# A mixture of 32 experts streamed from HBM: the fullest expert in one pass of 128 slots at a fixed place

## The reference

```python
def moe(h, w_router, b_router, w_gate, b_gate, w_up, b_up, w_down, b_down):
    logits = jnp.dot(h, w_router, preferred_element_type=jnp.float32) + b_router
    top_logit, top_idx = lax.top_k(logits, TOP_K)            # TOP_K = 4 of 32 experts
    gates = jax.nn.softmax(top_logit, axis=-1)
    ...
    def expert_block(args):                                  # xb: the tokens of one expert
        xb, e = args
        g = jnp.minimum(xb @ w_gate[e] + b_gate[e], SWIGLU_LIMIT)
        u = jnp.clip(xb @ w_up[e] + b_up[e], -SWIGLU_LIMIT, SWIGLU_LIMIT)
        act = g * jax.nn.sigmoid(SWIGLU_ALPHA * g) * (u + 1)
        return act @ w_down[e] + b_down[e]
    ...                                                      # sum over the 4 choices, times gate
```

## Time and profile before

| what | value |
|---|---|
| median of 3 runs | 1698.13 us (1698.03 to 1700.2) |
| profiled execution, span | 1695.8 us |
| PE busy | 1612.9 us, 95% |
| VectorE (DVE), ScalarE (ACT) busy | 392.1 us, 277.9 us |
| DMA | 524.72 MB, 309 GB/s over the span |
| granted TensorE clock, mean | 0.997 |

### The profile page before, as it was taken

One profiled execution on the slowest core, in us unless ns is written; L12 is line 12 of the kernel. 1 busy time (PEld: TensorE's weight loads), 2 busy tenths in 40 slices (PEclk: granted clock), 3 DMA queues, 4 the chain that ended last, 5 costly groups with the idle time before them and its releaser, 6 DMA issues.

```text
span 1695.8 us, 20330 instructions
## 1 busy us (share of the span) xinstructions
PE 1612.9 (95%) x8002; PEld 930.3 (55%) x8002; DVE 392.1 (23%) x839; ACT 277.9 (16%) x522; POOL 6.2 (0%) x15
## 2 busy tenths in 40 slices
PE   9999999999999999999999999999999999999987
PEld 8774878888888757843344333323333333333333
DVE  1444530322222222421212111112111111211112
ACT  2213122111112234310111101001110100101002
POOL 0000000000000000000000000000000000000000
PEclk9999999999999999999999999999999999999999
DMA  9526827344442234199999999999999999999994
GB/s 389 212 100 265 331 100 299 133 159 155 148 148 100 99 149 157 55 375 421 372 422 422 421 422 422 422 422 422 421 422 421 423 422 422 422 422 422 422 421 194
DMA packets 73341, 524.72 MB, mean 309 GB/s; under 512 B 8224, under 2 KB 8368, under 8 KB 9936
## 3 DMA queue, kind: packets, MB, share of 16 engines
q1 hardware_dynamic: 72432, 520.29, 75.6%
q0 software_dynamic: 864, 3.79, 0.6%
HBM read 522.99 MB, written 1.05 MB: 309 GB/s over the span
## 4 chain that ended last, share of the span: by engine, by line
PE 64%; DMA 31%; DVE 2%; ACT 1%; issue 1%; SPq 0%; ACTq 0%; DVEq 0%
PE bank L976 19%; DMA ring<-in_down_w 16%; DMA ring<-in_up_w 14%; PE bank L505 13%; PE bank L733 9%; PE bank L742 4%; PE bank L955 4%; PE bank L513 2%; PE bank L1009 2%; PE bank L520 2%; PE bank L610 1%; DMA ring<-in_front_w 1%; PE bank L993 1%; PE bank L535 1%; PE bank L563 1%; DVE squares L1485 1%
## 5 line engine op out<-in xcount | busy, mean ns | idle before, releaser
L976 PE MATMUL bank<-ring,probs_slab 128*64 128x512 f32 x3120 | 715.1, 599 | 37.0 <-DMA ring<-in_up_w 21.8
L976 PEld LDWEIGHTS bank<-ring,probs_slab 128*64 128x64 f32 x3120 | 207.5, 137 | 458.4 <-issue 358.2
L733 PE MATMUL bank<-normed,ring 128*128 128x256 f32 x704 | 153.7, 379 | 0.0
L733 PEld LDWEIGHTS bank<-normed,ring 128*128 128x128 f32 x704 | 133.7, 190 | 18.2
L1764 DVE TENSOR_TENSOR normed<-bank,big_slab 128x512 f32<-128x512 f32 x33 | 22.8, 692 | 494.4 <-PE bank L993 494.4
L505 PE MATMUL bank<-normed,ring 128*128 128x256 f32 x448 | 98.3, 380 | 0.0
L505 PEld LDWEIGHTS bank<-normed,ring 128*128 128x128 f32 x448 | 84.2, 190 | 13.1 <-ACT normed L1129 1.2
L1009 PE MATMUL bank<-mixed_slab,squares 64*128 64x256 f32 x528 | 65.9, 389 | 22.3 <-ACT squares L1362 22.3
L505 PE MATMUL bank<-mixed_slab,ring 128*128 128x256 f32 x384 | 83.6, 380 | 2.6 <-ACT mixed_slab L1148 2.6
L1607 DVE SCALAR_TENSOR_TENSOR big_slab<-bank,par,big_slab 128x255 f32<-128x255 f32 x88 | 42.4, 482 | 165.8 <-ACT big_slab L1250 157.4
L505 PEld LDWEIGHTS bank<-mixed_slab,ring 128*128 128x128 f32 x384 | 72.7, 190 | 13.3 <-issue 2.8
(11 more groups left out here) (270 smaller groups left out, 1124.0 us busy)
## 6 DMA issues: line engine op xcount, KB each, us to landing
ring<-in_down_w SPq DMA_DIRECT2D x132, 1024.0 KB, 25.1
ring<-in_up_w SPq DMA_DIRECT2D x130, 1024.0 KB, 26.3
ring<-in_gate_w SPq DMA_DIRECT2D x128, 1024.0 KB, 24.6
ring<-in_front_w SPq DMA_DIRECT2D x97, 1024.0 KB, 5.0
residual<-in_x SPq DMA_DIRECT2D x4, 256.0 KB, 6.7
memory_slab<-in_mem SPq DMA_DIRECT2D x1, 1024.0 KB, 15.9
context_slab<-in_ctx POOLq DMA_DIRECT2D x1, 1024.0 KB, 9.4
memory_slab<-in_gate_w SPq DMA_DIRECT2D x1, 1024.0 KB, 8.9
```

The lines of the kernel that those rows point to most:

```text
L733: mm = pe.matmul(bank[bank_at][:, half * T:(half + 1) * T], w[:, (half * DC + k) * P:(half * DC + k + 1) * P], H[:, k, :], start=(k == 0), ...
L976: mm = pe.matmul(to[half * SLOTS:(half + 1) * SLOTS, :], tokens(k), weights[:, i * D + half * HALF:i * D + (half + 1) * HALF], start=(k == ...
```

## The change

- The router's counts give the fullest of experts 0 to 28 (`movable`). Its index is worked out on VectorE, ahead of the search for extra items, and 64 is taken off its count.
- Experts are done in descending order: place p has expert 31 - p (`expert_at`). The fullest is put at place 16 (`DOUBLE`), and the expert whose place that was takes the place of the fullest. The order is a table in SBUF, `order_i`; SP and VectorE read it by register loads (`ordered`), SP after a wait for `s_order`.
- The item at place 16 has 128 slots: its tokens are 128 stationary columns, and each product fills a whole bank with each half of the outputs (`wide_product`). It uses all four free banks in turn. Its down product runs in the item at place 17 (`expert_after_double`). The pairs of places are regrouped around it, so that there are 17 gathers.
- SP's written-out loads cover places 0 to 2, whose experts are fixed (`STATIC`); all later ones come from its loop. The stashed chunks are now 8 to 13 in the order of use.
- The constant table has 196 more columns (1728 before).

The core of the diff; left out are the tables, semaphores and small buffers, the loops of ScalarE and of the extra items with their new counts, and VectorE's two corrections of the extra items' base.

```diff
-STASH, STASH_ITEM = 6, 4
-STASHED = range(2 * PART + (STASH_ITEM - 1) * ITEM_CHUNKS, 2 * PART + (STASH_ITEM - 1) * ITEM_CHUNKS + STASH)
-PEELED = STASH_ITEM + 1
-assert RING == ITEM_CHUNKS
+STASH = 6
+STASHED = range(2 * PART, 2 * PART + STASH)
+STATIC = 3
+DOUBLE = 16
+PAIRS = DOUBLE // 2 + 1 + (EXPERTS - DOUBLE) // 2
+PLACES = EXPERTS + 2
+assert RING == ITEM_CHUNKS and DOUBLE % 2 == 0 and STATIC < DOUBLE
+def expert_at(place):
+    return EXPERTS - 1 - place
...
+        wide_gate_n, wide_gate_f = flat(M, 0, 4), flat(M, 4, 4)
+        wide_up_n, wide_up_f = flat(VX, 0, 4), flat(VX, 4, 4)
+        wide_sig, wide_act = flat(KX, 0, 4), flat(KX, 4, 4)
+        wide_down_n = flat(PT, 0, 4)
...
-            for e in range(1, PEELED + 1):
-                opening += [(gate_w, e, c) for c in range(PART)] + [(up_w, e, c) for c in range(PART)]
-                opening += [(down_w, e - 1, c) for c in range(PART)]
+            for at in range(1, STATIC):
+                opening += [(gate_w, at, c) for c in range(PART)] + [(up_w, at, c) for c in range(PART)]
+                opening += [(down_w, at - 1, c) for c in range(PART)]
...
+            load_opening(range(STASHED.start))
             for i, at in enumerate(STASHED):
                 if i == 0:
                     full(sp, "qn2")
                     full(sp, f"a{LHEADS - 1}1")
                 elif i == 4:
                     full(sp, f"ao{LHEADS - 1}")
-                w, e, c = opening[at]
-                sp.dma_start(stash[i], w[e, c]).then_inc(stash_here[i], 16)
-            load_opening(range(RING - 4, RING))
-            load_opening(range(RING, STASHED.start))
+                w, place, c = opening[at]
+                sp.dma_start(stash[i], w[expert_at(place), c]).then_inc(stash_here[i], 16)
             load_opening(range(STASHED.stop, len(opening)))
-            with sp.Fori(PEELED + 1, EXPERTS) as e:
-                for part, w in enumerate((gate_w, up_w, down_w)):
+            sp.wait_ge(s_order, 1)
+            def ordered(place):
+                return sp.value_load(order_i[0:1, bass.ds(place, 1)], min_val=0, max_val=EXPERTS - 1)
+            with sp.Fori(STATIC, EXPERTS) as at:
+                now, before = ordered(at), ordered(at - 1)
+                for part, (w, e) in enumerate(((gate_w, now), (up_w, now), (down_w, before))):
                     for c in range(PART):
-                        sp.wait_ge(s_chunk, (e - 1) * ITEM_CHUNKS + (part * PART + c + 2 * PART + 1 - RING))
-                        load_part(w, e - 1 if part == 2 else e, c,
-                                  FRONT + 2 * PART + PART * part + c - STASH)
+                        sp.wait_ge(s_chunk, (at - 1) * ITEM_CHUNKS + (part * PART + c + 2 * PART + 1 - RING))
+                        load_part(w, e, c, FRONT + 2 * PART + PART * part + c - STASH)
+            last = ordered(EXPERTS - 1)
             for c in range(PART):
                 sp.wait_ge(s_chunk, EXPERT_CHUNKS - PART + c - RING + 1)
-                load_part(down_w, EXPERTS - 1, c, FRONT + 2 * PART + c - STASH)
+                load_part(down_w, last, c, FRONT + 2 * PART + c - STASH)
...
+            def wide_product(banks, tokens, first, turns):
+                for c in range(PART):
+                    n = FRONT + first + c - STASH
+                    pe.wait_ge(chunk_here[n % RING], 16 * (n // RING + 1))
+                    weights = ring[:, n % RING, :]
+                    for i in range(2):
+                        k = 2 * c + i
+                        for half in range(2):
+                            mm = pe.matmul(banks[half][:, :], tokens(k),
+                                           weights[:, i * D + half * HALF:i * D + (half + 1) * HALF],
+                                           start=(k == 0), stop=(k == DC - 1))
+                    mm.then_inc(s_chunk, 1)
+            def turn_wide(of, banks, done):
+                for j in range(DC):
+                    mm = pe.transpose(banks[j // 4][:, (j % 4) * P:(j % 4 + 1) * P],
+                                      of[:, j * P:(j + 1) * P], ident)
+                mm.then_inc(done, 1)
+            wide_tokens = lambda k: XS[:, k, :]
+            wide_operand = lambda k: wide_act[:, k * P:(k + 1) * P]
+            def chunk_of(e):
+                return 2 * PART + (e - 1) * ITEM_CHUNKS
+            def double_expert(e):
+                first, pair_at = chunk_of(e), e // 2
+                pe.wait_ge(s_xs, 2 * pair_at + 2)
+                pe.wait_ge(s_up_n, e)
+                wide_product((bank_gate, bank_up), wide_tokens, first, None)
+                pe.wait_ge(s_up_b, e)
+                wide_product((bank_down, bank_turn), wide_tokens, first + PART, None)
+                pe.wait_ge(s_gate_n, e + 1)
+                turn_wide(wide_gate_n, (bank_gate, bank_up), s_gate_t)
+                pe.wait_ge(s_up_n, e + 1)
+                pe.wait_ge(s_ea, e)
+                expert_product(bank_down, activated(1), range(4), first + 2 * PART, None)
+                pe.wait_ge(s_weighted, e)
+                pe.wait_ge(s_gate_b, e + 1)
+                turn_weights()
+                turn_wide(wide_up_n, (bank_turn, bank_up), s_up_t)
+                combine(e)
+                gather(pair_at + 1, lambda: pe.wait_ge(s_up_b, e + 1))
+            def expert_after_double(e):
+                first, pair_at = chunk_of(e), (e + 1) // 2
+                pe.wait_ge(s_xs, 2 * pair_at + 2)
+                expert_product(bank_gate, member(0), range(4), first, None)
+                expert_product(bank_up, member(0), range(2), first + PART, None)
+                pe.wait_ge(s_gate_n, e + 1)
+                turn_blocks(gate_n, s_gate_t)
+                expert_product(bank_up, member(0), range(2, 4), first + PART, None)
+                pe.wait_ge(s_weighted, e)
+                turn_weights()
+                pe.wait_ge(s_up_n, e + 1)
+                pe.wait_ge(s_gate_b, e + 1)
+                turn_blocks(up_n, s_up_t)
+                pe.wait_ge(s_ea, e)
+                pe.wait_ge(s_up_b, e + 1)
+                wide_product((bank_down, bank_turn), wide_operand, first + 2 * PART, None)
+                pe.wait_ge(s_down_n, e)
+                pe.wait_ge(s_gtev, e)
+                for c in range(DC):
+                    mm = pe.matmul(total[c // 2][:, (c % 2) * T:(c % 2 + 1) * T],
+                                   wide_down_n[:, c * P:(c + 1) * P], GT[:, :],
+                                   start=False, stop=True, skip_group_check=True)
+                mm.then_inc(s_comb, 1)
+            for e in range(1, STATIC):
...
+            with pe.Fori(STATIC // 2, DOUBLE // 2 - 1) as g:
                 expert(g * 2 + 1, 1, g * 2, 2 * PART, g + 1)
-                expert(g * 2 + 2, 0, g * 2, 2 * PART + ITEM_CHUNKS, None)
+                expert(g * 2 + 2, 0, g * 2, 2 * PART + ITEM_CHUNKS, None, g * 2 + 4)
+            expert(DOUBLE - 1, 1, None, chunk_of(DOUBLE - 1), DOUBLE // 2)
+            double_expert(DOUBLE)
+            expert_after_double(DOUBLE + 1)
+            with pe.Fori(0, (EXPERTS - DOUBLE) // 2 - 1) as g:
+                expert(g * 2 + DOUBLE + 2, 1, g * 2 + DOUBLE + 1, 2 * PART, g + DOUBLE // 2 + 2)
+                expert(g * 2 + DOUBLE + 3, 0, g * 2 + DOUBLE + 1, 2 * PART + ITEM_CHUNKS, None,
+                       g * 2 + DOUBLE + 6)
...
+            def double_expert(e):
+                act.wait_ge(s_chunk, e * ITEM_CHUNKS)
+                act.activation(wide_gate_n[:, 0:HALF], bank_gate[:, :], ACT.Copy)
+                act.activation(wide_gate_n[:, HALF:D], bank_up[:, :], ACT.Copy).then_inc(s_gate_n, 1)
+                act.wait_ge(s_chunk, e * ITEM_CHUNKS + PART)
+                act.activation(wide_up_n[:, 0:HALF], bank_down[:, :], ACT.Copy)
+                act.activation(wide_up_n[:, HALF:D], bank_turn[:, :], ACT.Copy).then_inc(s_up_n, 1)
+                act.wait_ge(s_gate_f, e + 1)
+                act.activation(wide_sig, wide_gate_f, ACT.Sigmoid, scale=ALPHA).then_inc(s_sig, 1)
+                down(e * ITEM_CHUNKS + 2 * PART)
+                tokens(e // 2 + 1)
+            def expert_after_double(e):
+                gate_and_up(e, e * ITEM_CHUNKS, e * ITEM_CHUNKS + PART)
+                act.wait_ge(s_chunk, e * ITEM_CHUNKS + 2 * PART)
+                act.activation(wide_down_n[:, 0:HALF], bank_down[:, :], ACT.Copy)
+                act.activation(wide_down_n[:, HALF:D], bank_turn[:, :], ACT.Copy).then_inc(s_down_n, 1)
             tokens(0)
             gate_and_up(0, PART, 2 * PART)
...
+            def pick_wide(e):
+                for t in range(2):
+                    ins = dve.tensor_scalar(PICK[:, t, :], const("slots"), rank[:, t, bass.ds(e, 1)],
+                                            None, ALU.is_equal)
+                ins.then_inc(s_picked, 1)
...
+            def add_bias(to, banks, b, e, done):
+                for half in range(2):
```

(76 more changed lines are left out.)

55 lines of the change are left out of this document (37 added, 18 removed).

## The result

The changed kernel takes 1680.89 us (median of 4, 1678.69 to 1684.13), the kernel before 1699.16 in the same comparison: ratio 0.9894, 95% interval 0.9882 to 0.9906. That is 18.3 us or 1.1% faster, inside the stated range of 1667 to 1684, and 6.5 us slower than the forecast of 1674.4. It lies outside the narrower range of 1671 to 1679 that the sum gave to its own case. The profiled execution has a span of 1678.5 us, where 1672.1 was forecast.

A forecast was written before the change was run, and what follows sets the result against it. The prediction took the weight stream to set the end of the expert stage. Span 1695.8 − 33.5 (extra item) + 8.8 (stash) + 1.0 (wide pair) = 1672.1 us; the median lies 2.3 above, so 1674.4 us, range 1667 to 1684.

The forecast's parts named there:

- the sum: Whole kernel: 1695.8 − 33.5 + 8.8 + 1.0 = 1672.1 us of span, 1674.4 us as median; own range 1671 to 1679.
- three signs of being wrong: Stream dips over 2 us after the wide pair; PE never waits for data afterwards; closing work exceeds 15.3 us.
- rival C: End of kernel: skipping the extra loop costs a code transfer, 5.2 us exposed, giving 1679.6 us; chance 0.09.
- rival A: Wide pair overruns the ring, stalling the stream; with 8 us more stalls, 1682.4 us; chance 0.16.
- What bounds the kernel: Expert stage: the weight stream sets the end, so each microsecond of stream idle after 722 costs one at the end.
- Part 1: After the ordinary experts: the extra item goes, saving 33.5 us.
- Part 2: Early expert stage: the moved stash makes the stream stand still 15.7 us against 6.9, so 8.8 us later.
- Part 3: Wide expert's pair: 79.6 us of PE, 19.9 more than the stream needs; 1.0 us of stream idle, bounds 0 and 8.
- the room in the ring: At the wide pair: some 21 us of other loads ahead of a load, so a lag of 19.9 just fits.
- Part 4: Finding the fullest, order reads, larger table and end-of-kernel skip: all costed at nothing.
- The skip: End of kernel: each engine skips the extra loop, costed at 0, bounds 0 and 5.2 us.

The follow-up runs named there:

- places 8 and 24: Two runs: changed kernel with the fullest expert at place 8 or 24 instead of 16; 1680.91 us and 1683.67 us.
- half the wide products: Changed kernel with only the first half of the wide products' outputs, so half of expert 1's results is left out; 1676.1 us.
- SP without the table: Changed kernel with SP taking the place number as the expert number instead of reading the order table; 1681.17 us.
- late-stash runs: Two runs: changed kernel with the stash back at chunks 44 to 49, the second with SP's written-out loads one item longer; 1673.86 and 1671.73 us.
- long skip: Kernel before without its extra item, with 64 more warming products in the unrun loop body; one execution, closing work 19.5 us.
- the kernel before without its item: Kernel before with the number of extra items set to 0, leaving out the last 31 tokens of expert 1; 1665.75 us.
- the last run: Changed kernel, stash at chunks 44 to 49, longer written-out SP loads, PE's last two experts written out of the loop; 1666.6 us.
- short body: Changed kernel with PE's unrun extra-item loop body cut to one warming product, read and branch kept; 1680.87 us, a single execution.
- without the branch: Changed kernel with the read of the extra-item count, the branch and its loop removed on PE alone; 1678.0 us.

## Why the forecast held, and where it was off

The median fell into the wide range, but two of the three signs of being wrong that the prediction named came true: the stream dips by 2.9 us after the wide pair (limit 2), and the closing work is 17.7 us (15.3). The wide range held because it had room for rival C and a part of A. No two errors cancelled: all were to the slow side.

1. **What bounds the kernel.** Right. Pauses of the stream appear at the end one for one, to 0.3 us: 12.7 us more standstill (19.6 against 6.9) moved the last combine from 1647.01, where it would be without the extra item, to 1660.78. Of the remaining 1.1, 0.5 are the stream's first microseconds (251 GB/s against 273 in 720 to 730; the stage starts 0.4 us later, 720.05 for 719.64), 0.3 are shortfalls of a few GB/s in single stretches (with them the standstill is 20.1 against 7.1), and 0.3 are open. One reading was wrong: I took 1034, where the chain has the issue of a load, for PE's first wait for data in the kernel before. That wait is at 1055.76; the sum doesn't use it. The changed kernel's first wait, forecast near expert 9 or 10, comes in place 8.
2. **Part 1.** Right: 33.5 us forecast, 32.6 measured alone.
3. **Part 2.** Right in place and kind, 1.0 us short in the profile: 16.7 us of pause for the 15.7 worked out from the releases. One possible cause is visible. The working took the release times of the kernel before; during the pause PE's own speed sets them, and the granted clock differs there. Counted from 720 to 760, so that an early or late start of the stream is in it, the executions with a granted clock of 1.00 in 740 to 750 (places 8 and 24) stand still for 15.1 and 15.3 us, those with 0.83 to 0.84 (changed kernel, half the wide products, SP without the table) for 16.3 to 16.9, and those with 0.68 to 0.76 for 17.2 to 18.9. I didn't vary the clock by itself, so the cause isn't shown.
4. **Part 3.** The PE cost is right to 0.2 us: 79.6 forecast, 79.4 measured. The step that failed is the room in the ring. I took 21 us, the median time from issue to landing less 5; 2.9 us of pause at a lag of 79.4 − 59.7 = 19.7 mean that it was about 17. The load issued behind the first wide chunk, at 1176.60, took 22.1 us to landing and not 26, which less 5 is 17.1; one at 1164.40 took 24.3, and those from 1144 to 1163 25.5 to 27.8. So the median hides the load with the least in front of it, and rival A came true in a small size. That this load sets the room fits these rows, but no run varies it alone. PE waited for data again in place 25 (1459.80), where 27 was forecast: the pause forgave 2.9 us of the lag, and the one more gather comes later than that.
5. **Part 4.** VectorE ends the search at 729.15 instead of 726.13, 2.6 us of it for the new steps and 0.4 for the later start, and its wait for PE shrank from 4.65 to 2.04 us, as forecast. The reads are hidden. The skip is the step that failed most: costed at 0 with a bound of 5.2, because PE's queue was to run ahead of its array and hide it, it took 2.4 us of closing work in the profiled execution, with PE idle for 2.77 us right behind the last combine. Rival C had a chance of 0.09 and the right mechanism, with 5.2 us as its size (2.4 or 4.3 measured); it came on top of the forecast case, not in its place.

Together: the last combine ends 4.0 us later than the 1656.8 (1672.1 − 15.3) of the forecast, 1.0 by the first pause, 1.9 by the second, 0.5 by the stream's first microseconds and 0.6 by the shortfalls and what is open. With 2.4 of skip these are the 6.4 us by which the span missed.

## What to carry to other kernels

Where a stream sets the end, count the microseconds in which it stands still, not those that an engine works: here a buffer held outside the ring cost 10 us for being used 36 chunks earlier, and a PE lag of 20 us cost 3. Keep such buffers for a time when the ring has been refilled, and check that waits written for the steady state also hold for the first round after them. A skip over a few hundred instructions near the end can cost nothing or up to 4.3 us by its position in the program, so look for a wait for nothing behind it, and at the clock after it.

## What the runs showed of the hardware that I had not expected

**The skip.** A branch over code that isn't run stalls PE by 2.4 to 2.9 us, or not at all. The distance alone doesn't decide: the changed kernel (2.77 us) and the run with half the wide products (no stall) skip the same code. The position does. Counted in the compiled programs, branch and target stand at PE's instructions 9092 and 9471 in the changed kernel, SP without the table and places 8 and 24, at 9655 and 10034 in both late-stash runs, and at 8436 and 9067 in the long skip, all seven with a stall. They stand at 8996 and 9375 with half the wide products, at 8436 and 8811 in the kernel before without its item, at 10218 and 10597 in the last run, and 9 instructions apart with the short body, all without one. In blocks of 256, the size in the rule cited above, every stall has its target two blocks on and none of the others has, if the blocks begin 22 to 72 instructions ahead of the multiples of 256. That shift is fitted, so this is an estimate; my rougher count behind the expectation of the last run differed by about one block and led to the same forecast there.

The traces show the transfers too. In all seven stalls the queue that the profile calls "instruction" moves a block of 0.02 MB 0.1 to 0.2 us before the last combine ends, and the next one 3.0 to 3.4 us behind that end, some 0.5 us after PE runs again. In the three longer skips without a stall the first of the two is there (0.1 us before to 0.1 after) and the second isn't; without the branch, and with the short body, there is none. That fits a wait for code; what passes between the first transfer and PE's start 2.4 to 2.9 us later the traces don't show. The stall is exposed because the branch comes behind the last combine, with nothing left to hide it.

**The clock behind it.** After such a stall PE's closing products ran at half the granted clock in five profiled executions (long skip, both late stashes, places 8 and 24; closing work 19.2 to 19.5 us) and at the full clock in two (the changed kernel, 17.7; SP without the table, 17.4). Before it PE had been idle for 2.4 to 2.9 us in all seven. Without the stall the clock stayed at 1.00 while PE worked, and the closing work was 15.2 to 15.4 us in all five executions. So the skip costs 2.4 us or 4.3.
